# Latent attention: the sums of squares over the channels as two fp32r products with ones, in place of one full-precision product

## The reference

```python
def rms_norm(x, gain=None):
    xf = x.astype(jnp.float32)
    y = xf * lax.rsqrt(jnp.mean(xf * xf, axis=-1, keepdims=True) + RMS_EPS)
...
    qh = (rms_norm(m_q, q_a_norm) @ w_q_up).reshape(B, S, MLA_HEADS, MLA_NOPE + MLA_ROPE)
    q_nope, q_pe = qh[..., :MLA_NOPE], qh[..., MLA_NOPE:]
    q_nope = rms_norm(q_nope, q_norm_nope)
    q_pe = apply_rope(rms_norm(q_pe, q_norm_rope), cos[:, :, None, :], sin[:, :, None, :])
    kv = (rms_norm(m_kv, kv_a_norm) @ w_kv_up).reshape(B, S, MLA_HEADS, MLA_NOPE + MLA_V)
    k_nope, mv = kv[..., :MLA_NOPE], kv[..., MLA_NOPE:]
    k_nope = rms_norm(k_nope, k_norm_nope)
    k_pe = apply_rope(rms_norm(m_kpe, k_norm_rope), cos, sin)
    mla_out = mla_attention(q_nope, q_pe, k_nope, k_pe, mv).reshape(B, S, D_MLA)
```

## Time and profile before

| | before |
|---|---|
| median of 3 runs | 4064.37 us (4064.3 to 4065.46) |
| profiled execution, its own time | 4064.26 us |
| its span, from the first to the last instruction | 4062.3 us |
| mean granted clock of TensorE over the span | 0.996 |
| PE busy | 4007.3 us, 99% of the span |
| DVE busy | 2204.5 us, 54% |
| ACT busy | 1476.3 us, 36% |
| POOL busy | 106.9 us, 3% |

### The profile page before, as it was taken

One profiled execution on the slowest core, in us unless ns is written; L12 is line 12 of the kernel. 1 busy time (PEld: TensorE's weight loads), 2 busy tenths in 40 slices (PEclk: granted clock), 3 DMA queues, 4 the chain that ended last, 5 costly groups with the idle time before them and its releaser, 6 DMA issues.

```text
span 4062.3 us, 47419 instructions
## 1 busy us (share of the span) xinstructions
PE 4007.3 (99%) x18798; PEld 3079.2 (76%) x18798; DVE 2204.5 (54%) x3451; ACT 1476.3 (36%) x2422; POOL 106.9 (3%) x170
## 2 busy tenths in 40 slices
PE   8999999999999999999999999999999999999998
PEld 5777657888888877656788888777777777887786
DVE  7877676534344656466634343553446363646664
ACT  4533464312212334545412121333434343324533
POOL 2000000000000000000000000000000000000000
PEclk9999999999999999999999999999999999999999
DMA  7534101233332321201222221231111111116542
GB/s 246 204 108 130 55 1 42 89 93 107 94 100 78 89 78 33 85 11 32 62 89 88 78 73 46 69 114 47 37 47 42 42 47 63 42 53 227 187 163 76
DMA packets 99621, 342.12 MB, mean 84 GB/s; under 512 B 11016, under 2 KB 12072, under 8 KB 98250
## 3 DMA queue, kind: packets, MB, share of 16 engines
q1 hardware_dynamic: 78522, 258.87, 19.7%
q0 software_dynamic: 20880, 80.23, 6.3%
HBM read 304.45 MB, written 34.60 MB: 83 GB/s over the span
## 4 chain that ended last, share of the span: by engine, by line
PE 87%; DVE 7%; ACT 3%; issue 2%; DMA 1%; SPq 0%; POOL 0%; DVEq 0%; ACTq 0%
PE PS L1297 35%; PE PS L1279 20%; PE PS L2385 4%; PE PS L2244 3%; PE PS L3281 2%; PE PS L3345 2%; PE PS L2154 1%; PE PS L1682 1%; PE PS L1262 1%; PE PS L1962 1%; PE PS L2675 1%; PE PS L2122 1%; PE PS L2702 1%; PE PS L2688 1%; PE PS L1968 1%
## 5 line engine op out<-in xcount | busy, mean ns | idle before, releaser
L639 ACT ACTIVATE WH<-raw 128x1024 fp32r<-128x1024 f32 x314 | 330.6, 1053 | 680.1 <-PE PS L1297 443.8
L1279 PE MATMUL PS<-hi,WH 128*128 128x512 f32 x1248 | 524.5, 420 | 0.4 <-DVE WL L650 0.2
L1297 PE MATMUL PS<-lo,WH 128*128 128x512 f32 x1312 | 515.5, 393 | 0.0
L1297 PE MATMUL PS<-hi,WH 128*128 128x512 f32 x1312 | 513.8, 392 | 1.3 <-DVE WL L650 0.7
L1297 PE MATMUL PS<-hi,WL 128*128 128x512 f32 x1312 | 513.3, 391 | 0.0
L1279 PE MATMUL PS<-hi,WL 128*128 128x512 f32 x1248 | 491.5, 394 | 0.0
L1279 PE MATMUL PS<-lo,WH 128*128 128x512 f32 x1248 | 488.7, 392 | 0.0
L650 DVE TENSOR_TENSOR WL<-raw,WH 128x1024 fp32r<-128x1024 f32 x274 | 335.0, 1222 | 127.6 <-ACT WH L639 127.5
L1297 PE MATMUL PS<-al,WH 128*128 128x512 f32 x768 | 302.3, 394 | 0.0
L1297 PE MATMUL PS<-ah,WH 128*128 128x512 f32 x768 | 301.7, 393 | 0.0
L1297 PE MATMUL PS<-ah,WL 128*128 128x512 f32 x768 | 298.9, 389 | 0.0
(11 more groups left out here) (472 smaller groups left out, 6940.0 us busy)
## 6 DMA issues: line engine op xcount, KB each, us to landing
adab<-in_w_ada POOLq DMA_DIRECT2D x120, 512.0 KB, 4.6
raw<-in_win SPq DMA_DIRECT2D x104, 512.0 KB, 3.6
raw<-in_down SPq DMA_DIRECT2D x80, 512.0 KB, 3.6
raw<-in_up SPq DMA_DIRECT2D x64, 512.0 KB, 3.6
raw<-in_dft SPq DMA_DIRECT2D x24, 512.0 KB, 4.0
sp_x<-X SPq DMA_DIRECT2D x24, 512.0 KB, 6.2
X<-sp_x SPq DMA_DIRECT2D x24, 512.0 KB, 4.8
raw<-in_wout SPq DMA_DIRECT2D x24, 512.0 KB, 3.7
```

Of the source, the lines that this page charges most:

```text
L639: act.activation(PLACES[PLACE[j]][0], raw[:, j % 2, :], ACT.Copy).then_inc(*W_HI.next(j))
L1279: mm = pe.matmul(bank[b + hf], w[:, k, :], r[:, k, HALF[hf]], start=k == 0 and w is wh and r is hi, stop=k == 7 and w is wl)
L1297: mm = pe.matmul(bank[b + hf], w[:, k, :], r[:, k, HALF[hf]], start=k == 0 and w is wh and r is hi, stop=k == 7 and w is wl)
```

## The change

For every norm unit with a single source ScalarE writes two squares: the fp32 square as before, and a second one in fp32r (`SPLIT[lane][1]`). VectorE subtracts the second from the first and writes the rest in fp32r (`SPLIT[lane][0]`). TensorE multiplies both by ones in fp32r and adds them in the same PSUM bank, in place of the one fp32 product. TensorE's wait is now for the subtraction. The two-source units of `mq` stay as they are. The program times of these units move: TensorE's product from +1 to +1.9, Ln from +2 to +2.6, VectorE's last steps from +4, +4.5 and +5.4 to +4.4, +5.0 and +5.8, the subtraction stands at +0.9, and a unit is longer in its lane by 0.5. `const_r`, `adab_r`, `pb_r` and `pT_r` are fp32r names for the memory of `const`, `adab`, `pb` and `pT`. The constants are rewritten once through `const_r` by one ScalarE copy of 128x512 at program time 50 (`ones_act`), for which TensorE waits once (`ones_pe`). The fp32 uses of the constants read the same memory by a bitcast. The two queues of transfers, their order and the activation tables that are loaded stay as they are.

```diff
@@ -338,10 +338,14 @@
         self.raw = sb(top, "raw", [P, 2, S])
         self.WH = sb(top, "WH", [P, 2, S], R)
         self.WL = sb(top, "WL", [P, 2, S], R)
+        with ExitStack() as c:
+            self.adab_r = sb(c, "adab_r", [P, 2, S], R)
+            sb(c, "gap3", [P, NVEC])
+            self.const_r = sb(c, "const_r", [P, 4, P], R)
         self.adab = sb(top, "adab", [P, 2, S])
         self.vecs = sb(top, "vecs", [P, NVEC])
         self.const = sb(top, "const", [P, 4, P])
-        self.ident, self.ones, self.onesbd, self.rotm = (self.const[:, i, :] for i in range(4))
+        self.ident, self.ones, self.onesbd, self.rotm = (self.const_r[:, i, :].bitcast(F) for i in range(4))
         self.negm = sb(top, "negm", [P, P])
         self.lmask = sb(top, "lmask", [P, 8, P], U8)
         self.cond = sb(top, "cond", [P, S])
@@ -401,6 +405,11 @@
                 self.st = sb(c, "st", [P, 7, P])
                 self.wg = sb(c, "wg", [P, 256])
                 self.el = sb(c, "el", [P, 8])
+            with ExitStack() as c:
+                sb(c, "gap5", [P, 9, S])
+                sb(c, "gap6", [P, HS])
+                self.pb_r = sb(c, "pb_r", [P, S + HS], R)
+                self.pT_r = sb(c, "pT_r", [P, 12, P], R)
             with ExitStack() as c:
                 self.wq = sb(c, "wq", [P, 2, 768])
 
@@ -1836,7 +1845,7 @@
             head: object = None
             late: bool = False
 
-        LONG = {"norm": 5.0, "newton": 7.5, "project": 2.5, "rotate": 3.5, "copy": 1.0, "exchange": 0.9, "values": 3.0}
+        LONG = {"norm": 5.5, "newton": 8.0, "project": 2.5, "rotate": 3.5, "copy": 1.0, "exchange": 0.9, "values": 3.0}
 
         def pair_at(l, h, p):
 
@@ -1933,6 +1942,18 @@
                    (m.pb[:, 0:HS], m.pb[:, HS:S])]
         SCRATCH.append(tuple(m.pT[:, 4 * x:4 * x + 4, :].rearrange("p a b -> p (a b)") for x in range(2)))
 
+        SPLIT = [(m.adab_r[:, 0, HALF[x]], m.adab_r[:, 1, HALF[x]]) for x in range(2)] + [(m.pb_r[:, 0:HS], m.pb_r[:, HS:S])]
+        SPLIT.append(tuple(m.pT_r[:, 4 * x:4 * x + 4, :].rearrange("p a b -> p (a b)") for x in range(2)))
+
+        def ones_act(act):
+            yield 50.0
+            act.wait_ge(*CONST[0])
+            act.activation(m.const_r[:, :, :], m.const[:, :, :], ACT.Copy).then_inc(*ML_ACT.next("ones"))
+
+        def ones_pe(pe):
+            yield FIRST_SUMS - 0.1
+            pe.wait_ge(*ML_ACT["ones"])
+
         def mla_sp(sp, l):
             yield out_at(l, 1) + 18
             sp.wait_ge(*GL_PE["out", l, 1, 1, 1])
@@ -1949,7 +1970,7 @@
             units = mla_units(l)[0][lane]
             b = 3 + lane
             for u in units:
-                yield u.at + (1 if u.kind in ("norm", "newton") else 0)
+                yield u.at + (0 if u.kind not in ("norm", "newton") else 1.9 if len(u.src) == 1 else 1)
                 if u.kind in ("copy", "exchange"):
                     continue
                 if u.i:
@@ -1957,6 +1978,13 @@
                 else:
                     pe.wait_ge(*GL_DVE["picked", l, 1, 6, 1])
                 if u.kind in ("norm", "newton"):
+                    if len(u.src) == 1:
+                        pe.wait_ge(*ML_DVE["rest", l, lane, u.i])
+                        mat = m.const_r[0:u.rows, 2 if u.mat is m.onesbd else 1, 0:u.rows]
+                        for x, a in enumerate(SPLIT[lane]):
+                            mm = pe.matmul(PS[0:u.rows, b, :], mat, a[0:u.rows, :], start=x == 0, stop=x == 1)
+                        mm.then_inc(*ML_PE.next(l, lane, u.i))
+                        continue
                     pe.wait_ge(*ML_ACT["square", l, lane, u.i])
                     for x, a in enumerate(SCRATCH[lane][:len(u.src)]):
                         mm = pe.matmul(PS[0:u.rows, b, :], u.mat[0:u.rows, 0:u.rows], a[0:u.rows, :], start=x == 0,
@@ -2007,8 +2035,10 @@
                         act.wait_ge(*W_MM[TILE_OF["win", l, 3][0]])
                     for x, a in zip(u.src, (s1, s2)):
                         sq = act.activation(a[0:u.rows, :], x[0:u.rows, HALF[u.hf]], ACT.Square, bias=0.0)
+                    if len(u.src) == 1:
+                        sq = act.activation(SPLIT[lane][1][0:u.rows, :], u.src[0][0:u.rows, HALF[u.hf]], ACT.Square, bias=0.0)
                     sq.then_inc(*ML_ACT.next("square", l, lane, u.i))
-                    yield u.at + 2
+                    yield u.at + (2.6 if len(u.src) == 1 else 2)
                     a1, a2 = s1[0:u.rows, :], s2[0:u.rows, :]
                     act.wait_ge(*ML_PE[l, lane, u.i])
                     act.activation(a1, PS[0:u.rows, b, :], ACT.Ln, bias=m.col[0:u.rows, 0:1], scale=1.0 / u.n).then_inc(
@@ -2035,7 +2065,13 @@
             for u in units:
                 a1, a2 = s1[0:u.rows, :], s2[0:u.rows, :]
                 if u.kind in ("norm", "newton"):
-                    yield u.at + (4 if u.kind == "norm" else 5.4 if u.late else 4.5)
+                    if len(u.src) == 1:
+                        yield u.at + 0.9
+                        dve.wait_ge(*ML_ACT["square", l, lane, u.i])
+                        high, low = SPLIT[lane][1][0:u.rows, :], SPLIT[lane][0][0:u.rows, :]
+                        dve.tensor_tensor(low, a1, high.bitcast(F), ALU.subtract).then_inc(
+                            *ML_DVE.next("rest", l, lane, u.i))
+                    yield u.at + (4.4 if u.kind == "norm" else 5.8 if u.late else 5.0)
                     if u.kind == "newton":
                         dve.wait_ge(*ML_ACT["again", l, lane, u.i])
                         dve.scalar_tensor_tensor(out=a2, in0=PS[0:u.rows, b, :], scalar=EPS * u.n, in1=a2, op0=ALU.add,
...
```

More of the change, by code:

```diff
@@ L553, in build @@
         FN_ACT, FN_DVE, OUT = signal("final_act"), signal("final_dve"), signal("out_stored")
-        SPARE = m.const[:, :, :].rearrange("p a b -> p (a b)")
+        SPARE = m.const_r[:, :, :].bitcast(F).rearrange("p a b -> p (a b)")
         def spare_pe(pe, b, n, x=SPARE):
@@ L755, in setup_sp @@
             sp.dma_start(m.w4[:, :, :, :].rearrange("p a b c -> p (a b c)"), D["fw4"]).then_inc(*W4_IN.next(0, by=16))
-            for dst, name in ((ident, "ident"), (ones, "ones"), (m.onesbd, "onesbd"), (m.rotm, "rotm"), (m.negm, "negm")):
-                sp.dma_start(dst[:, :], D[name]).then_inc(*CONST.next(0, by=16))
+            for i, name in enumerate(("ident", "ones", "onesbd", "rotm", "negm")):
+                sp.dma_start(m.const[:, i, :] if i < 4 else m.negm[:, :], D[name]).then_inc(*CONST.next(0, by=16))
             sp.dma_start(m.fso[0:1, 0, :, :], D["fbias"]).then_inc(*FBIAS_IN.next(0, by=16))
@@ L3516, in pe_program @@
         def pe_program(pe):
-            in_order(setup_pe(pe), filters_pe(pe), filter_spectra_pe(pe), *norms(first_norm_pe, half_norm_pe, pe), spare_norm_pe(pe), *per_layer(win_first_pe, pe), *per_layer(win_pe, pe),
+            in_order(setup_pe(pe), filters_pe(pe), filter_spectra_pe(pe), ones_pe(pe), *norms(first_norm_pe, half_norm_pe, pe), spare_norm_pe(pe), *per_layer(win_first_pe, pe), *per_layer(win_pe, pe),
                      *per_layer(win_values_pe, pe), *per_layer(gla_decays_pe, pe), *per_layer(gla_levels_pe, pe),
@@ L3534, in act_program @@
             in_order(weights_act(act), setup_act(act), setup_weights_act(act), filters_act(act), filter_spectra_act(act), first_squares_act(act),
-                     *norms(first_norm_act, half_norm_act, act), *per_layer(win_act, act), rope_act(act), *per_layer(mixer_table, act),
+                     ones_act(act), *norms(first_norm_act, half_norm_act, act), *per_layer(win_act, act), rope_act(act), *per_layer(mixer_table, act),
                      *per_layer(gla_decays_act, act), *per_layer(gla_outputs_act, act), *per_layer(gla_squares_act, act),
```

## The result

The changed kernel takes 4129.44 us (median of 4 runs, 4121.36 to 4130.76), the kernel before 4064.91 (4 runs, 4064.3 to 4067.52). The ratio is 1.0153, with a 95% interval from 1.0141 to 1.0165: slower by 1.5%, 65 us, outside the range of the prediction. The profiled execution took 4129.03 us, with a span of 4127.2.

The account below looks back on a forecast made before the run. TensorE was taken as the bound, its products in this stage without reserve behind their squares. Waits of 29.65 us a layer, less 9.6 saved and 3.65 already waited, give +16.4, +32.8 for two layers: 4064.3 + 32.8 = 4097, range 4072 to 4114.

Parts of the forecast that it names:

- The saving: On TensorE, 24 single-source units a layer, each 0.40 us cheaper as two fp32r products: 19.2 us, 9.6 a layer.
- The sum of the waits: TensorE's waits in the opening and heads 1 to 3: 9.7 + 5.95 + 7.0 + 7.0 = 29.65 us a layer.
- First keys units: Head 3's, walked: squares and subtraction take 4.4 us, TensorE has cover of 1.9, so it waits 2.5.
- Last keys units of heads 2 and 3: The second keys unit: VectorE's mask and softmax steps, subtraction and late Newton steps come first; TensorE waits 3.35 us.
- First `mkv` unit: Opening: its squares need a `misc` step now behind the third `wol`; TensorE waits 3.7 us, before 0.18.
- First `misc` unit: Opening of a layer: TensorE waits 1.3 us ahead of this unit.
- Output projection: Opening: TensorE waits 2.2 us, as the bank's `X` step stands behind the `pT` subtraction and four `mq` steps.
- The second queries unit: Head 3: subtraction behind the `wol` splitting, 0.65 us, and transpositions waiting for the `pT` copy, 0.95; together 1.6.
- likeliest case: Waits as walked through the stage's units: +33 us, 4097, own range 4084 to 4108; chance 0.62.
- Waits hidden, faster: The engines' orders fit so that the stage stays bound by TensorE's work: 4045 us; chance 0.07.
- Only the direct waits: Keys units and 6 products without reserve wait, some late steps are absorbed: 16 us a layer, 4070 us; chance 0.17.
- The clock falls too: TensorE's clock drops behind three waits a layer of 3.3 us and more, 2.8 each: 4114 us; chance 0.14.

## Why the prediction was wrong

- **The saving** was 0.40 for each of 48 units, 19.2 us. Measured 0.86 less 0.47, and the page's PE busy agrees to half a microsecond once the clock is taken off.
- **The sum of the waits** was 29.65 a layer less the 3.65 of before, 52.0 in all. Measured 53.4. By these two terms alone the kernel would take 4064.4 + 53.4 - 19.2 = 4098.6, and the forecast was 4097. With the clock held up by spare products it took 4103.5.
- **Single terms.** First keys units 2.5: measured 2.34, three times a layer. Last keys units of heads 2 and 3, 3.35 each: 3.34 and 3.98. First `mkv` unit 3.7: 3.22. First `misc` unit 1.3: 1.10. Output projection 2.2: 1.90. Two were wrong. The second queries unit was to wait 1.6, since the subtraction was to stand behind `wol`; it stands ahead of it in the order, and what is left is 0.41 at the products with the values in head 2 and nothing in head 3. And the projection of `mkv` in the opening, which waits 2.42, was not walked: its `mkv` step had moved behind the splitting of `WL` on VectorE. The error of one paid for the other, so the right sum is in part luck. Three smaller slips moved little: by the ends of the squares and the starts of the products, 13 of the 28 products of a layer, and not 18, follow within 0.2 us; the terms of the first `mkv` unit add up to 3.8; and the fall of the earlier trace rows reaches into the next window and lost 3.4 us, not 2.8.
- **The step that failed** is the price of TensorE's clock. The text had "Waits of 3.3 us and more are three a layer in my walk", "6 x 2.8 = 17", and gave this rival 0.14 beside a likeliest case without it. The runs have 31 to 32.5 us, in 14 stretches. The mechanism was right, and two of its numbers were not. The number of places: the clock fell also behind waits of 2.34, 2.07 and 1.90, so that nine waits a layer were candidates and not three. And the chance: the one fall of the earlier trace rows was read as a special case "beside transfers". The trace before has two more behind waits that the text did not look at, one behind a wait of 3.16 at 71.92 us, and this one:

```profile
320.09 0.74 PE L1366 MATMUL PS<-const,vf 128*128 128x128 f32 x4 [2.28 <-DVE VT L1397]
```

```profile
320.00:324.00 4.00, 3.91 (x18) 2.91 (x18) 4.00 (x6) 0.51 (x2) 0.28 (x1) 0.57 0.40 157
```

A wait of 2.28 was followed by 0.57 in the kernel before, with a DMA share of 0.40 and not of 1.03 as in the earlier trace rows; this row would have put the waits of 2.34 among the candidates. 4097 + 31 = 4128, and 4129.44 was measured. The Trainium skill, "TensorE: Matmul & The Clock Gate", section "Why this matters for your kernels", names idle gaps between bursts of matmuls as what brings the lower clock back. The runs agree in kind: with the gaps filled the mixers stand at 1.00 but for one stretch, with open ones at 0.50 behind most of them.
- **The rivals.** "Waits hidden, faster" and "Only the direct waits" have fallen: they had at most 13.25 and 16 us of waits a layer, and the runs have 53.4 / 2 + 3.65 = 30.4. "The clock falls too" had the right mechanism and half of its price.
- **Where the time went, by runs:** the order +17.5, the second square and the cheaper products -8.1, the subtraction +55.7, of which 28.4 is waiting and the rest nearly all clock. These are steps in this sequence and no fixed prices: with the whole split in place the order is worth only 4129.4 - 4124.9 = 4.5.
- **What stays open:** which waits are followed by a fall. The same wait of 2.34 was in one head and not in the next; in the run with the times of before, one of 3.09 was followed by none, while 1.54 was enough in the run without the subtraction. So the cost of a given wait is known as a mean over many only. The runs of one kernel, up to 10 us apart, go with it: with the times of before under the split, the run of 4116.07 has a mean granted clock of 0.995, the three of 4124.5 and more have 0.992.

## What to carry to other kernels

Where the bound engine waits for short chains through other engines, first ask how early the operands are there; with a slack of 0.15 us, a step of 0.69 on an engine that is half idle costs its full length, and the queue ahead of it as well. A cheaper product is a gain when the chain in front of it stays as short as it was: one square in fp32r, with the rest of the square left out, gave 26 us, and the split in two lost 65. And price TensorE's new waits above their length where they are as long as those that a fall followed here, 1.54 to 3.98 us: 53 us of new waits cost another 31.

## What the runs showed of the hardware that was not expected

In the mixers a fall of the granted clock came in portions: each of the 14 stretches of the change cost 1.7 us or 3.4 us, as did those of every other run. And the same wait can have a fall behind it or not. The wait of 2.28 at 320 us stands in all 14 kernels, at 2.28 to 2.32; in 9 of the profiled executions a fall follows, as in the kernel before, and in 5 none, as in that with all these products in fp32r:

```profile
319.96 0.63 PE L1375 MATMUL PS<-const_r,vf 128*128 128x128 f32 x4 [2.30 <-DVE VT L1406]
```

```profile
320.00:324.00 4.00, 4.00 (x43) 3.39 (x44) 4.00 (x7) 1.63 (x3) 0.42 (x1) 1.00 0.41 164
```

In the run with the times of before TensorE waited 3.09 us ahead of a unit, and no fall followed (its timeline, and its windows with the columns of the earlier trace rows):

```profile
577.69 0.70 PE L1985 MATMUL PS<-adab_r,const_r 128*128 128x512 f32 x2 [3.09 <-DVE adab_r L2072]
```

```profile
574.00:578.00 4.00, 0.91 (x4) 0.49 (x3) 3.88 (x7) 2.19 (x4) 0.00 (x0) 1.00 0.01 2
578.00:582.00 4.00, 4.00 (x24) 2.51 (x23) 2.08 (x4) 2.21 (x4) 0.00 (x0) 1.00 0.00 0
```

And spare products, which are pure work for the bound engine, made the kernel 26 us faster.
